# A gated recurrence with decays, roots and inputs of its own for either direction, its first convolution tap on ScalarE, and the next weights split in other places

## The reference, cut to what matters

```python
    u = centred_depthwise_conv(u, conv_w[l], conv_b[l])       # 4 taps, tokens t-2 .. t+1
    h_fwd = rg_lru(u, w_rg_a[l, 0], b_rg_a[l, 0], w_rg_i[l, 0], b_rg_i[l, 0], lru_lambda[l, 0], False)
    h_bwd = rg_lru(u, w_rg_a[l, 1], b_rg_a[l, 1], w_rg_i[l, 1], b_rg_i[l, 1], lru_lambda[l, 1], True)
    y_rec = ((h_fwd + h_bwd) * jax.nn.gelu(y_branch)) @ w_rec_o[l]

def rg_lru(u, w_a, b_a, w_i, b_i, lam, reverse):
    r_gate = jax.nn.sigmoid(block_diag_linear(u, w_a, b_a)).astype(jnp.float32)
    i_gate = jax.nn.sigmoid(block_diag_linear(u, w_i, b_i))
    log_a = -LRU_C * r_gate * jax.nn.softplus(-lam.astype(jnp.float32))
    a = jnp.exp(log_a)
    mult = jnp.sqrt(jnp.maximum(-jnp.expm1(2.0 * log_a), 0.0))
    bx = mult * (i_gate * u).astype(jnp.float32)
    # h[t] = a[t] * h[t-1] + bx[t], over the tokens forwards or backwards
```

## Time and profile before

| | |
|---|---|
| median of 3 runs | 3903.18 us (3898.33 to 3904.03) |
| profiled execution | 3904.28 us |
| its span, first to last instruction | 3902.5 us |
| TensorE busy | 3683.4 us, 94% |
| VectorE busy | 1849.4 us, 47% |
| ScalarE busy | 1121.0 us, 29% |
| mean granted clock of TensorE | 0.97 |
| the recurrence, from tile 0's gates to job 18's first matmul | 378.35 to 658.60 us |

### The profile page before, as it was taken

How to read it: one execution, slowest core, us unless ns; L and a number is a source line. 1 busy time by engine, 2 the same in 40 slices (tenths; PEclk the granted TensorE clock), 3 DMA queues, 4 the chain that set the end, 5 groups by cost and what they waited for, 6 DMA issues and landing times. The chain is left out here.

```text
span 3902.5 us, 45791 instructions
## 1 busy us (share of the span) xinstructions
PE 3683.4 (94%) x18128; PEld 2752.1 (71%) x18128; DVE 1849.4 (47%) x3366; ACT 1121.0 (29%) x1863; POOL 702.2 (18%) x533
## 2 busy tenths in 40 slices
PE   8989889999999999999996898998899989999998
PEld 4456666886588888877555777655788558888886
DVE  2086776221277455434447898358521142223232
ACT  1055665210221122113333333117521032222110
POOL 1064000011010111101002010006501113333333
PEclk9999999999999999997997998899999999999999
DMA  3000111113023223222001111300012211111111
GB/s 144 3 18 16 36 36 39 49 49 113 27 91 104 87 91 99 76 83 95 27 6 30 39 38 36 126 17 1 16 47 69 80 43 44 50 48 48 50 54 43
DMA packets 260097, 211.61 MB, mean 54 GB/s; under 512 B 65584, under 2 KB 222896, under 8 KB 259504
## 3 DMA queue, kind: packets, MB, share of 16 engines
q1 hardware_dynamic: 258128, 201.61, 16.6%
q10 hardware_dynamic: 1760, 7.08, 0.8%
HBM read 185.33 MB, written 21.50 MB: 53 GB/s over the span
## 5 line engine op out<-in xcount | busy, mean ns | idle before, releaser
L95 PE MATMUL ps<-halves 128*128 128x512 f32 x9408 | 2165.0, 392 | 53.2 <-DVE halves L507 28.0
L95 PEld LDWEIGHTS ps<-halves 128*128 128x128 f32 x9408 | 1776.6, 189 | 433.1 <-issue 48.2
L95 PE MATMUL ps<-arena 128*128 128x512 f32 (+2 forms) x1296 | 504.9, 548 | 3.8 <-DVE arena L354 2.9
L95 PEld LDWEIGHTS ps<-arena 128*128 128x128 f32 x1296 | 246.5, 208 | 224.8 <-issue 215.3
L1430 POOL TENSOR_TENSOR tmps<-tmps 128x512 f32<-128x512 f32 x128 | 142.4, 1113 | 1012.2 <-ACT tmps L1398 1012.2
L1451 DVE TENSOR_TENSOR halves<-tmps,halves 128x512 fp32r<-128x512 f32 x128 | 89.3, 698 | 450.8 <-ACT halves L1406 450.8
L1335 ACT ACTIVATE halves<-raws 128x2048 fp32r<-128x2048 f32 x62 | 118.4, 1909 | 593.9 <-PE ps L95 532.5
L1437 POOL TENSOR_TENSOR arena<-arena 128x512 f32<-128x512 f32 x128 | 164.7, 1294 | 191.3 <-DVE arena L1478 191.3
L95 PE MATMUL ps<-arena,tokens 128*128 128x512 f32 (+1 forms) x512 | 195.3, 540 | 0.0
L1026 POOL TENSOR_TENSOR arena<-arena 128x512 f32<-128x512 f32 x32 | 47.7, 1490 | 805.4 <-DVE arena L1011 556.9
L1398 ACT ACTIVATE tmps<-ps 128x512 f32<-128x512 f32 x128 | 76.6, 598 | 381.3 <-PE ps L95 381.3
(11 more groups left out here) (291 smaller groups left out, 3632.0 us busy)
## 6 DMA issues: line engine op xcount, KB each, us to landing
raws<-in_w_ff SPq DMA_DIRECT2D x31, 1024.0 KB, 6.2
raws<-in_w_mlp SPq DMA_DIRECT2D x31, 1024.0 KB, 5.2
mixw<-in_w_in SPq DMA_DIRECT2D x48, 512.0 KB, 4.0
arena<-in_w_ada SPq DMA_DIRECT2D x48, 512.0 KB, 3.8
arena<-in_w_in SPq DMA_DIRECT2D x8, 2048.0 KB, 12.7
arena<-in_x SPq DMA_DIRECT2D x8, 1024.0 KB, 8.4
arena<-in_w_out SPq DMA_DIRECT2D x4, 2048.0 KB, 11.3
h_stash<-arena SPq DMA_DIRECT2D x1, 5120.0 KB, 20.2
```

The source lines that it names most:

```text
L95: ins = e.matmul(out_ap, l, r, start=i == 0, stop=i == n - 1)
```

## The change

- `a_`, `s_`, `iu_` and the scans' outputs exist once for each direction; the output buffer `hs_[dd]` also holds the squared decay (`t2_` before). The evictions of direction dd wait for the scan of the same direction of the tile before (`r_h.at(t * 2 + dd - 1)` in place of `r_h.at(t * 2 + dd)`).
- `ub` and the y buffer exist once. The evictions of u(t) wait for the taps of t - 1, those of y(t) for the y step of t - 1.
- The first tap, `cw * u + cb`, is an Identity activation on ScalarE behind the evictions of u, with VectorE's waits for the output's place; VectorE waits for it (`r_lm`) and does the other three taps.
- ScalarE's order is: gates 0, copy of the y weights, gates 1, gelu tanh, root 0, root 1, u and first tap of t+1, copy of the u weights of t+2, y of t+1.
- VectorE's order is: argument 0, split of the y weights, argument 1, y step, forward scan, taps of t+1, split of the u weights of t+2, backward scan, sum, output, gelu steps of t+1.
- Branch 0's load waits for the y product of tile 7 instead of its y step; the buffers of the first mix outputs are renumbered, and the third, not the fourth, waits for the last output of the recurrence.

```diff
-        ub = [R(B0 + i * 1032, 1028) for i in range(2)]
-        uc_, y_, t1_, a_, s_, iu_, hf_ = (R(rb + i * 1024, 1024) for i in range(7))
-        ys = [y_.rearrange("p (r q) -> p r q", q=64), R3(20480, 16, 64)]
+        ub = R(F2, 1028)
+        uc_, y_, t1_, a0, s0, iu0, h0_, a1, s1, h1_, iu1 = (R(F2 + 1028 + i * 1024, 1024) for i in range(11))
+        a_, s_, iu_, hs_ = (a0, a1), (s0, s1), (iu0, iu1), (h0_, h1_)
+        y3 = y_.rearrange("p (r q) -> p r q", q=64)
...
             for t in range(8):
                 scalar_rec_gates(e, t, 0)
+                scalar_weights(e, 2 * t + 3)
+                scalar_rec_gates(e, t, 1)
                 e.wait_ge(*r_g1.at(t + 1))
                 e.activation(t1_, t1_, ACT.Tanh, scale=GC).then_inc(*r_g2.tick())
-                scalar_weights(e, 2 * t + 3)
-                scalar_rec_root(e, t, 0)
-                scalar_rec_gates(e, t, 1)
                 if t == 7:
                     scalar_branch(e, 0)
+                scalar_rec_root(e, t, 0)
+                scalar_rec_root(e, t, 1)
                 if t < 7:
                     scalar_rec_u(e, t + 1)
-                scalar_rec_root(e, t, 1)
-                if t < 7:
+                    scalar_weights(e, 2 * t + 4)
                     scalar_rec_y(e, t + 1)
-                    scalar_weights(e, 2 * t + 4)
...
-                if t >= 2:
-                    e.wait_ge(*r_uc.at(t - 1))
-                e.activation(ub[t % 2][:, 2 + n0:2 + n0 + N], bk.tile(key)[:, :], ACT.Identity,
+                if t:
+                    e.wait_ge(*r_uc.at(t))
+                e.activation(ub[:, 2 + n0:2 + n0 + N], bk.tile(key)[:, :], ACT.Identity,
                              bias=V("bu", t)).then_inc(*bk.emptying(key))
+            e.wait_ge(*bk.clear(("u", t, 1)))
+            if t >= 2:
+                e.wait_ge(*r_h.at(t * 2 - 2))
+                e.wait_ge(*bk.full(("rg", t - 2, 1, 1, 1)))
+            e.activation(ucs[t % 2], r16(ub[:, 0:1024]), ACT.Identity, scale=V("cw", t),
+                         bias=V("cb", t)).then_inc(*r_lm.tick())
...
-                    if t or dd:
-                        e.wait_ge(*r_h.at(t * 2 + dd))
+                    if t:
+                        e.wait_ge(*r_h.at(t * 2 + dd - 1))
...
-            e.tensor_scalar(o, r16(u[:, 0:1024]), cw(0), V("cb", t), ALU.mult, ALU.add).then_inc(*dv.tick())
+            e.wait_ge(*r_lm.at(t + 2))
             for j in range(1, 4):
-                e.wait_ge(*dv.now())
+                if j > 1:
+                    e.wait_ge(*dv.now())
...
             for t in range(8):
                 vector_rec_arg(e, t, 0)
+                vector_weights(e, 2 * t + 3)
+                vector_rec_arg(e, t, 1)
                 e.wait_ge(*r_g2.at(t + 1))
...
-                vector_weights(e, 2 * t + 3)
-                vector_rec_scan(e, t, 0)
-                vector_rec_arg(e, t, 1)
                 if t == 7:
                     vector_branch(e, 0)
+                vector_rec_scan(e, t, 0)
                 if t < 7:
                     vector_rec_conv(e, t + 1)
+                    vector_weights(e, 2 * t + 4)
                 vector_rec_scan(e, t, 1)
...
                 if t < 7:
                     vector_rec_gelu(e, t + 1)
-                    vector_weights(e, 2 * t + 4)
...
-            if x < 2:
-                e.wait_ge(*(r_h.at(16) if x else r_y.at(8)))
+            if x == 1:
+                e.wait_ge(*r_h.at(16))
+            elif x == 0:
+                e.wait_ge(*bk.full(("y", 7, 1)))
...
-                elif u == 3:
+                elif u == 2:
                     e.wait_ge(*r_rc.at(8))
```

More of the change, by code:

```diff
@@ L695, in sync_rec_gates @@
             g = gw[t % 2]
-            e.wait_ge(*r_zero.at(6))
+            e.wait_ge(*r_zero.at(4))
             if t >= 2:
@@ L760, in scalar_rec_gates @@
         def scalar_rec_gates(e, t, dd):
-            for w, (dst, bo) in enumerate(((a_, dd * 8 + t), (iu_, 16 + dd * 8 + t))):
+            for w, (dst, bo) in enumerate(((a_[dd], dd * 8 + t), (iu_[dd], 16 + dd * 8 + t))):
                 for h, (n0, N) in enumerate(HALVES):
@@ L771, in scalar_rec_gates @@
             e.wait_ge(*bk.clear(("rg", t, dd, 0, 1)))
-            e.activation(s_, a_, ACT.Tanh, scale=kp, bias=kp).then_inc(*av.tick())
+            e.activation(s_[dd], a_[dd], ACT.Tanh, scale=kp, bias=kp).then_inc(*av.tick())
             e.wait_ge(*av.now())
-            e.activation(a_, a_, ACT.Exp, scale=kn, bias=kn).then_inc(*r_ex.tick())
+            e.activation(a_[dd], a_[dd], ACT.Exp, scale=kn, bias=kn).then_inc(*r_ex.tick())
         def scalar_rec_root(e, t, dd):
             e.wait_ge(*r_sa.at(t * 2 + dd + 1))
-            e.activation(s_, s_, ACT.Sqrt, scale=0.25).then_inc(*r_sq.tick())
+            e.activation(s_[dd], s_[dd], ACT.Sqrt, scale=0.25).then_inc(*r_sq.tick())
         def vector_rec_arg(e, t, dd):
             e.wait_ge(*r_ex.at(t * 2 + dd + 1))
-            e.tensor_tensor(t2_, a_, a_, ALU.mult).then_inc(*dv.tick())
+            e.tensor_tensor(hs_[dd], a_[dd], a_[dd], ALU.mult).then_inc(*dv.tick())
             e.wait_ge(*dv.now())
-            e.scalar_tensor_tensor(out=s_, in0=t2_, scalar=1.0, in1=s_, op0=ALU.add,
+            e.scalar_tensor_tensor(out=s_[dd], in0=hs_[dd], scalar=1.0, in1=s_[dd], op0=ALU.add,
                                    op1=ALU.mult).then_inc(*r_sa.tick())
@@ L789, in vector_rec_scan @@
             e.wait_ge(*bk.clear(("rg", t, dd, 1, 1)))
-            e.scalar_tensor_tensor(out=r16(iu_), in0=r16(iu_), scalar=1.0, in1=ucs[t % 2], op0=ALU.add,
+            iu, h = iu_[dd], hs_[dd]
+            e.scalar_tensor_tensor(out=r16(iu), in0=r16(iu), scalar=1.0, in1=ucs[t % 2], op0=ALU.add,
                                    op1=ALU.mult).then_inc(*dv.tick())
@@ L793, in vector_rec_scan @@
             e.wait_ge(*r_sq.at(t * 2 + dd + 1))
-            e.tensor_tensor(iu_, iu_, s_, ALU.mult).then_inc(*dv.tick())
+            e.tensor_tensor(iu, iu, s_[dd], ALU.mult).then_inc(*dv.tick())
             e.wait_ge(*dv.now())
[L796 to L800, removed]
+            step = 1 if dd == 0 else -1
+            e.tensor_tensor_scan(h[:, ::step], a_[dd][:, ::step], iu[:, ::step], 0.0, ALU.mult,
+                                 ALU.add).then_inc(*r_h.tick())
         def vector_rec_conv(e, t):
-            u, o = ub[t % 2], ucs[t % 2]
+            o = ucs[t % 2]
             cw = lambda j: V("cw", j * 8 + t)
[L805 to L808, removed]
-            e.tensor_scalar(o, r16(u[:, 0:1024]), cw(0), V("cb", t), ALU.mult, ALU.add).then_inc(*dv.tick())
+            e.wait_ge(*r_lm.at(t + 2))
             for j in range(1, 4):
-                e.wait_ge(*dv.now())
-                e.scalar_tensor_tensor(out=o, in0=r16(u[:, j:j + 1024]), scalar=cw(j), in1=o, op0=ALU.mult,
+                if j > 1:
+                    e.wait_ge(*dv.now())
+                e.scalar_tensor_tensor(out=o, in0=r16(ub[:, j:j + 1024]), scalar=cw(j), in1=o, op0=ALU.mult,
                                        op1=ALU.add).then_inc(*(r_uc if j == 3 else dv).tick())
@@ L860, in vector_rec @@
                     vector_rec_gelu(e, t + 1)
-                    vector_weights(e, 2 * t + 4)
         MX = R3(F2, 8, 1024)
-        tmpx = [R(CB + 1024 + i * 512, 512) for i in (2, 3, 4, 0, 1)]
+        tmpx = [R(o, 512) for o in (51456, 51968, 49920, 50432, 50944)]
         tmpy = [R(20480 + i * 512, 512) for i in range(4)]
```

32 lines of the change are left out of this document (14 added, 18 removed).

## The result

| | before | after |
|---|---|---|
| median | 3902.98 us (3898.33 to 3904.03, 4 runs) | 3861.61 us (3857.36 to 3865.94, 4 runs) |
| profiled execution | 3904.28 us | 3860.55 us |
| span | 3902.5 us | 3858.4 us |

The ratio is 0.9896, with a 95% interval of 0.9879 to 0.9913. In a second comparison, the changed kernel beside the kernel before on one chip, it was 0.9884 (0.9870 to 0.9899), 3860.98 against 3904.50 us.

The account below looks back on a forecast made before the run. The prediction took VectorE's 34.48 us round to bound the recurrence; with TensorE's 28.80 us round instead, job 18 starts at 614.34 instead of 658.60, 44.26 us earlier. From the median, 3903.18 - 44.3 = 3858.9 us, range 3852 to 3874.

Parts of the forecast that it names:

- 6.24 us wait: VectorE's wait each round for ScalarE's backward exp before the backward decay; forecast to fall to about 1.4 us.
- The round: Time between two tiles' gate matmuls in the recurrence: 28.80 us, TensorE's floor, instead of 34.48 us.
- The join: Job 18's weights arrive 0.4 us before TensorE wants them, so it starts at 614.34 instead of 658.60, 44.26 us earlier.
- R: Start of the gate matmuls of a tile, from which the prediction's walk counts times in us.
- All of it shifts: Behind 658.60 us, loads are released by TensorE's own progress, so the later stages move earlier by the whole gain.
- (1): Own buffers for either direction: backward evictions wait for the previous tile's scan, so VectorE's 6.24 us wait goes.
- (2): Both roots side by side: one pair of table loads a tile instead of two, 2 x 1.30 us less on ScalarE.
- (4): y weights copied and split before the backward gates, u weights before ScalarE's y evictions and VectorE's backward scan; nothing late.
- (3): First tap moves to ScalarE: VectorE saves 0.84 us a round, ScalarE gains one 128x1024 activation.
- Rival A: VectorE or ScalarE stays the recurrence's bound, with part of the gain: 3870.5 or 3884 us; chance 0.13.
- Rival B: Backward gates still run late, so only the tap and the loads are saved, 15 us: 3888 us; chance 0.02.
- Rival C: ScalarE stalls on the u weights' load; slower if it lands over 21.3 us after issue, 3929 at 25; chance 0.05.

Follow-up runs that it names:

- Buffers alone: The changed kernel's separate buffers and relaxed wait, with both engines' orders and the tap as before; 3864.17 us against 3904.97 us for the kernel before.
- extra products: The changed kernel with four more unused VectorE products of 128x1024 behind each tile's gelu steps; 3884.73 us.
- y jobs with two products: The changed kernel with one of three products (high weights by low input) left out in the recurrence's y jobs; 3844.96 us.
- weight steps back: The changed kernel with the two weight copies and two weight splits back in their old places in the queues; 3866.84 us.
- root early: The changed kernel with the forward root ahead of the backward gates again on ScalarE, a table load before and after it; 3897.88 us.
- tap back: The changed kernel with the first tap back on VectorE; 3855.97 us, then 3858.53 us beside the changed kernel's 3860.98 us.
- tap alone: The kernel before with only its first tap moved to ScalarE; 3898.19 us against 3904.97 us.
- late load: The changed kernel with the load of the u weights of tile t+2 waiting until y of t+1 is done; 3882.28 us.

## Why the prediction was right

Forecast 3858.9 us, range 3852 to 3874; measured 3861.61.

**The bound and the wait.** Right. The 6.24 us wait became 1.26 (forecast 1.35) and TensorE the bound, with no idle time at all. Buffers alone show that the shared buffers were the cause of most of it. The extra products and the y jobs with two products show the slack of VectorE from both sides, 1.35 us in either run.

**The round.** 28.80 was forecast and 28.64 measured. The term was taken from one start to the modelled end of the next stretch, which overlaps the gates' start by about 0.15 us; seven times that is 1.1 us.

**The join.** Forecast 44.26 us up to job 18, measured 45.9: the 1.1 of the rounds, 0.2 of an earlier start (378.11 against 378.35) and 0.3 of the same modelled end in the last stretch, reckoned as 6.46 + 27.93 = 34.39 and measured as 612.7 - 578.59 = 34.1. The weights of job 18 were ready at R+33.5 (612.08 - 578.59) where 33.94 was reckoned, and bound neither sum: the 0.4 us to spare there were 0.7.

**From the stage to the time.** Here the forecast was 2.7 us too low. The stage brought 1.6 more than forecast, the span 0.2 less than the 44.3, and the medians differ by 41.4. Of this, 2.4 us are the place of the two profiled executions in their own spreads: 1.3 above the median before, 1.1 below it after. "All of it shifts" was right for the order of the work and not for each stage's length. Behind job 18 TensorE was busy 3.3 us longer than before (3102.9 against 3099.5) and idle 1.5 us less (142.8 against 144.4), so the prediction's one term for the stages behind, no change, was off by 1.8 us. A forecast can't be closer than this scatter; that it came within 3 us is in part luck.

**The clock.** Right: 1.00 in the recurrence, where 0.90 and 1.00 took turns in the kernel before.

**Edit by edit.** (1) The buffers are worth about 41 us by the times and 37.7 by the start of job 18. (2) and (4), the orders, are worth the rest: 3 to 6 us by the times, 8 to 11 by the start of job 18. What (2) is worth without (4) no run shows; weight steps back, which keeps (2), begins job 18 later than buffers alone, which has neither. The prediction counted (2) as 2 x 1.30 us of ScalarE's time, which is the wrong ledger. ScalarE had time to spare; the place of the root matters because, with VectorE's new order, a root ahead of the backward gates ties the two engines into one loop of 33.5 us. The root early shows it, and with VectorE's old order the root stood there too, in rounds of 29.5 on average (buffers alone). (3) The tap was given 0.84 us a round of VectorE's slack and no time, and the sentence on the rule that would leave it on VectorE said that the round would be 28.3 and still under TensorE's. That is what the tap back showed; the rule from the Trainium skill, "ScalarE: Activation LUTs", Rules for kernel authors, would have been as good here, and 6.8 us worse in the kernel before (tap alone).

**The table load's price.** The load took 1.28 us and the next activation began 1.29 after its start (477.71 to 479.00); the activation ahead of it ended at 477.69. That is about half of the 2.66 that the Trainium skill, "ScalarE: Activation LUTs", What ACT_TABLE_LOAD costs, gives for a switch with the drain. The row decided rightly.

**Rival A** did not come: with 27.29 us in the y jobs with two products VectorE runs its own work and no more. **Rival B** did not come. **Rival C** had no effect at the landing times of this kernel: ScalarE waits at most 1.9 us for the load at this place. Its price was not tested. It priced a late load by L + 2.3 + 10.9, the loop from one u's end to the next. In the late load, issued 11.17 us late and landed 4.07 us on, L is 15.2 and that loop 28.4, no longer than the round. The 31.8 us measured are those of the loop through the y split and the y matmuls, which the experiment itself made by hanging the issue on y's end. A load that is issued at u's end, as in the changed kernel, and only lands late does not close that loop, and no run had one. So the 21.3 us of the prediction stay an estimate.

## What to carry to other kernels

Walk one round of the pipeline, engine by engine, with start-to-start steps from the trace, and close every loop: the bound is the longest of TensorE's own round, each other engine's own round and each loop that passes between engines, and the slack to the second longest says what a further edit is worth. A buffer that two phases share can force the work of two engines into a line, here for 6.24 us a round; and once it is split, the order of the queues decides which loops exist, so a step moved ahead of another's wait can give nearly the whole gain back (the root early, 37 of 43.5 us). Work moved off an engine counts only while that engine is the bound: the same tap was worth 6.8 us in one kernel and nothing in the other. And read an edit's worth where it acts: the times of whole executions scatter here by some us with TensorE's clock, while the round was 28.64 in four executions out of four (changed and tap back, twice each).

## What the runs showed of the hardware that was not expected

A table load of ScalarE can run ahead of the wait of the activation that needs it. With the root early it ran at 483.35 us, while the root itself began at 489.56, after 4.92 us of waiting for VectorE, so a load in front of a wait for another engine can be free. It is not always so: in the kernel before, the load ahead of the gates began only when the scan had released ScalarE. Both have their waits written ahead of the activation, the root one (VectorE's argument) and the gates two (the bank, filled by TensorE, and the scan). The trace of the root early tells these two apart, by ScalarE's timeline:

```profile
505.21 1.28 ACT L772 ACT_TABLE_LOAD   x1
...
511.19 0.69 ACT L772 ACTIVATE arena<-ps,hb 128x512 f32<-128x512 f32 x1 [4.69 <-PE ps L689]
```

The scan that these gates wait for had ended at 505.14; the gate matmuls that fill the bank began only at 509.10. So the load passed the wait for the bank, and in the kernel before it was held by the one for the scan, when the bank was full. Why one is passed and the other not, no run shows.
